# Two attention loops of a two-block network on one core: how operands of 64 and 15 rows are laid out for TensorE

## The reference

```python
def stick_breaking_attention(q, k, v):                 # q, k, v: 8 heads of 64
    for i in range(s_len // Q_BLOCK):                  # two blocks of 128 queries
        z = jnp.einsum('bhqd,bhkd->bhqk', qb, kb).astype(jnp.float32) * scale
        log_1m = jnp.where(mask, jax.nn.log_sigmoid(-z), 0.0)
        suffix = lax.cumsum(log_1m, axis=3, reverse=True) - log_1m
        a = jnp.where(mask, jnp.exp(jax.nn.log_sigmoid(z) + suffix), 0.0)
        outs.append(jnp.einsum('bhqk,bhkd->bhqd', a.astype(vb.dtype), vb))
```

```python
        logit_c = jnp.einsum('bqghd,bngd->bqghn', qt, k_cmp).astype(jnp.float32) + bias_c[None]
        p_c = jax.nn.softmax(logit_c, axis=-1) * has_any[None, :, None, None, None]
        o_c = jnp.einsum('bqghn,bngd->bqghd', p_c.astype(v_cmp.dtype), v_cmp)   # n = 15
        ...
        o = gt[..., 0:1] * o_c + gt[..., 1:2] * o_s + gt[..., 2:3] * o_w
```

## Time and profile before

| | |
|---|---|
| median of 3 runs | 1212.1 us (1211.89 to 1212.76) |
| the profiled execution | 1208.83 us, its trace spans 1207.0 us |
| PE busy with matmuls | 1192.6 us, 99% of the span |
| DVE, ACT, POOL busy | 861.1, 646.8, 216.9 us |
| the chain that ended last | 93% PE, 3% DVE, 2% DMA, 1% ACT |
| granted TensorE clock, mean | 0.998 of full speed |
| DMA | 182 GB/s over the span, queue 1 takes 49.6% of the 16 engines |
| a turn of the first head loop | 7.84 to 8.20 us |
| a turn of the NSA loop | 5.14 us |

### The profile page before, as it was taken

How to read it: one execution, slowest core, us unless ns; L and a number is a source line. 1 busy time by engine, 2 the same in 40 slices (tenths; PEclk the granted TensorE clock), 3 DMA queues, 4 the chain that set the end, 5 groups by cost and what they waited for, 6 DMA issues and landing times.

```text
span 1207.0 us, 19811 instructions
## 1 busy us (share of the span) xinstructions
PE 1192.6 (99%) x7931; PEld 1066.7 (88%) x7931; DVE 861.1 (71%) x1188; ACT 646.8 (54%) x868; POOL 216.9 (18%) x106
## 2 busy tenths in 40 slices
PE   8999999999999999999999999999999999999997
PEld 6888889988899888888999988888899879888886
DVE  6887666788767787766778777665688776766553
ACT  6655545465655665544643555544446774655441
POOL 0444300000000244310000025510000330454000
PEclk9999999999999999999999999999999999999999
DMA  8555545953335455555545555555567205555540
GB/s 301 189 210 179 205 175 179 277 208 106 105 139 185 159 210 190 185 199 181 179 163 179 194 189 208 182 202 181 201 246 268 82 1 175 210 179 203 180 170 36
DMA packets 31570, 217.55 MB, mean 180 GB/s; under 512 B 3584, under 2 KB 3856, under 8 KB 6272
## 3 DMA queue, kind: packets, MB, share of 16 engines
q1 hardware_dynamic: 30144, 210.85, 49.6%
q0 software_dynamic: 1344, 5.53, 1.6%
HBM read 215.30 MB, written 4.22 MB: 182 GB/s over the span
## 4 chain that ended last, share of the span: by engine, by line
PE 93%; DVE 3%; DMA 2%; ACT 1%; issue 0%; SPq 0%; DVEq 0%; ACTq 0%
PE bank L1514 38%; PE bank L1515 19%; PE bank L1507 9%; PE bank L1508 9%; PE bank L1509 9%; DMA raw<-weights 1%; DVE w_hl L792 1%; PE bank L1891 1%; PE bank L1603 1%; DMA h<-x_t 1%; PE bank L1605 1%; PE bank L1604 1%; ACT w_hl L405 1%; PE bank L1789 1%; PE bank L1777 0%
## 5 line engine op out<-in xcount | busy, mean ns | idle before, releaser
L792 DVE TENSOR_TENSOR w_hl<-raw,w_hl 128x2048 fp32r<-128x2048 f32 x194 | 444.0, 2289 | 117.5 <-ACT w_hl L405 116.5
L405 ACT ACTIVATE w_hl<-raw 128x2048 fp32r<-128x2048 f32 x195 | 370.4, 1902 | 116.7 <-PE bank L1515 50.8
L1514 PE MATMUL bank<-x_hl,w_hl 128*128 128x512 f32 x864 | 301.2, 394 | 1.8 <-DVE w_hl L1010 0.9
L1514 PE MATMUL bank<-hidden,w_hl 128*128 128x512 f32 x832 | 288.6, 393 | 0.0
L361 POOL TENSOR_TENSOR hidden<-hid_f,hidden 128x256 fp32r<-128x256 f32 (+1 forms) x76 | 188.1, 2474 | 525.3 <-ACT hidden L488 309.7
L1515 PE MATMUL bank<-x_hl,w_hl 128*128 128x256 f32 x864 | 240.5, 278 | 0.0
L1515 PE MATMUL bank<-hidden,w_hl 128*128 128x256 f32 x832 | 231.0, 278 | 0.0
L1514 PEld LDWEIGHTS bank<-x_hl,w_hl 128*128 128x128 f32 x864 | 161.9, 187 | 39.7 <-DVE w_hl L792 1.2
L1514 PEld LDWEIGHTS bank<-hidden,w_hl 128*128 128x128 f32 x832 | 155.9, 187 | 35.8
L1507 PE MATMUL bank<-x_hl,w_hl 128*128 128x256 f32 x576 | 164.6, 286 | 0.1
L1508 PE MATMUL bank<-x_hl,w_hl 128*128 128x256 f32 x576 | 162.9, 283 | 0.0
(11 more groups left out here) (360 smaller groups left out, 1598.6 us busy)
## 6 DMA issues: line engine op xcount, KB each, us to landing
raw<-weights SPq DMA_DIRECT2D x197, 1024.0 KB, 4.9
bias_skew<-bias_rows POOLq DMA_DIRECT2D x1, 3072.0 KB, 27.7
gate_or_bias<-bias_skew POOLq DMA_DIRECT2D x1, 2048.0 KB, 10.7
h<-x_t SPq DMA_DIRECT2D x2, 512.0 KB, 6.4
raw<-weights SPq DMA_DIRECT2D x2, 512.0 KB, 8.3
out_t<-out_g SPq DMA_DIRECT2D x4, 256.0 KB, 2.5
con<-consts SPq DMA_DIRECT2D x1, 769.5 KB, 13.5
heads<-p_t POOLq DMA_DIRECT2D x1, 256.0 KB, 2.7
```

What stands on the lines that cost most here:

```text
L405: nc.scalar.activation(dst, src, ACT.Copy).then_inc(hi_split, 1)
L792: V.tensor_tensor(w_lo[:, s, :], raw[:, s, :], w_hi[:, s, :].bitcast(F32), ALU.subtract).then_inc(lo_split, 1)
L1514: mm(out_, w_hi[:, s, c:c + m], x, start=start, stop=False, **kw)
```

## The change

Stick-breaking queries now lie in tiles of 128 partitions with zeros in the rows of the other head: even heads in `sb_q` (in `y_f`), with partitions 64 to 127 zero, odd heads in two new tiles `sb_odd`, with partitions 0 to 63 zero. The tiles `sb_odd` use memory of `y_hl` that is free at that time. The keys stay two heads to a tile. `z` of a head is then a product over all 128 partitions. POOL writes the zeros once, after the last chunk of the first feed-forward layer. DVE writes the queries with two instructions of 64 partitions in place of one of 128; the keys take a plain product with the scale. In the head loop, `z` now stands ahead of the MLA scores.

In the NSA layer `v_cmp` grows from 64 to 256 columns, filled with zeros by POOL, and group `g` writes its 15 rows in columns 64 `g` to 64 `g` + 63. Part 2 of `n_out` then uses all 128 partitions of `v_cmp` and `c_t`.

```diff
@@ -165,6 +165,8 @@
         f_at = nc.sbuf_base
         x_f, y_f = sb("x_f", [P, KT, S]), sb("y_f", [P, KT, S])
         blk_k = nc.alloc_sbuf_tensor_at("blk_k", [P, 16, 2, 64], F32R, offset=f_at)
+        sb_odd = [nc.alloc_sbuf_tensor_at(f"sb_odd{i}", [P, 2, S], F32, offset=nc.sbuf_base + (5 + 2 * i) * 2 * S * 4)
+                  for i in range(2)]
         y_hl = sb("y_hl", [P, KT, 2, S], F32R)
 
         hidden = nc.alloc_sbuf_tensor_at("hidden", [P, 2 * MF, 2, S], F32R, offset=over)
@@ -218,6 +220,7 @@
             sem("s_z"), sem("s_abs"), sem("s_min"), sem("s_ln"), sem("s_l"), sem("s_e"), sem("s_x"), sem("s_a"),
             sem("s_pv"))
         merged_done = sem("merged_done")
+        masks = sem("masks")
         ple_sig = sem("ple_sig")
         bias_ready, bias_out, bias_in = sem("bias_ready"), sem("bias_out"), sem("bias_in")
         bias_mm = sem("bias_mm")
@@ -262,7 +265,7 @@
         s_t2, s_m, s_lm = (sq_flat[:, 384 * i:384 * i + 384] for i in range(3))
         s_p = [sq_flat[:, 1152 + 384 * i:1536 + 384 * i] for i in range(2)]
 
-        v_cmp = mv[:, 0, 0:64]
+        v_cmp = mv[:, 0, 0:256]
         c_stat = mv[:, 1, 160:288].rearrange("p (a q h) -> p a q h", a=4, q=2)
 
         k_cmp = mv[:, 1, 0:64].rearrange("p (j e n) -> p j e n", j=2, e=2)
@@ -362,6 +365,10 @@
                                             ALU.subtract).then_inc(hid_lo, 1)
 
             low("ffn1")
+            pool.wait_ge(chunk_used, C["latent"])
+            nc.gpsimd.memset(sb_q[64:128, :, :], 0.0).then_inc(masks, 1)
+            for t in sb_odd:
+                nc.gpsimd.memset(t[0:64, :, :], 0.0).then_inc(masks, 1)
             pool.wait_ge(bias_ready, 1)
             pool.dma_start(bias_rows.ap(), bias_1d[:, :]).then_inc(bias_out, 16)
             pool.wait_ge(bias_out, 16)
@@ -384,6 +391,7 @@
             nc.gpsimd.memset(blk_k[:, :, :, 60:64].bitcast(F32), 0.0).then_inc(setup, 1)
             nc.gpsimd.memset(blk_v[:, :, :, 60:64].bitcast(F32), 0.0).then_inc(setup, 1)
             pool.wait_ge(op_lo, PC["blk_v"] + 1)
+            nc.gpsimd.memset(v_cmp, 0.0).then_inc(setup, 1)
             nc.gpsimd.memset(y_flat[:, 0:1024], 0.0).then_inc(setup, 1)
             for t in range(PAIRS - 1):
                 pool.wait_ge(n_fac, t + 1)
@@ -1054,8 +1062,14 @@
                 c = C["sb_q"] + j
                 dve.wait_ge(chunk_used, c + 1)
                 b = two(bank[:, TURN + (DRAIN["sb"] + j) % 3, :])
-                V.scalar_tensor_tensor(out=y_f[:, 2 * j:2 * j + 2, :], in0=b, scalar=0.125 if j < 2 else 1.0,
-                                       in1=r_two, op0=ALU.mult, op1=ALU.mult).then_inc(drained, 1)
+                if j < 2:
+                    dve.wait_ge(masks, 3)
+                    for rows, q in ((slice(0, 64), sb_q[0:64, 2 * j:2 * j + 2, :]), (slice(64, 128), sb_odd[j][64:128, :, :])):
+                        ins = V.scalar_tensor_tensor(out=q, in0=b[rows], scalar=0.125, in1=r_two[rows], op0=ALU.mult,
+                                                     op1=ALU.mult)
+                else:
+                    ins = V.tensor_tensor(y_f[:, 2 * j:2 * j + 2, :], b, r_two, ALU.mult)
+                ins.then_inc(drained, 1)
                 nxt(c)
             rsqrt("c_q", bank[:, SUMS, 0:S], width=384, r_out=r_lat[:, 0, :])
             rsqrt("c_kv", bank[:, 3, 0:S], width=256, r_out=r_lat[:, 1, :], last=r_ready)
@@ -1427,9 +1441,10 @@
                 src = bank[rows, 0, 256:288].rearrange("p (a b) -> p a b", a=2)
                 ins = V.tensor_copy(k_cmp[rows, :, e, 0:NCMP], src[:, :, 0:NCMP])
             ins.then_inc(cmp_done, 1)
+            dve.wait_ge(setup, 8)
             for g in range(4):
                 rows = slice(32 * g, 32 * g + NCMP)
-                ins = V.tensor_copy(v_cmp[rows, :], bank[rows, 0, 320:384])
+                ins = V.tensor_copy(v_cmp[rows, 64 * g:64 * g + 64], bank[rows, 0, 320:384])
             ins.then_inc(cmp_done, 1)
             nxt(PHI[3])
             n_factors(0)
@@ -1437,7 +1452,7 @@
             c_max, c_sum, c_rec, c_fac = (c_stat[:, m, :, :] for m in range(4))
             by_head = lambda ap: ap.rearrange("p (t g) -> p t g", t=4)
             dve.wait_ge(c_scores, 1)
-            dve.wait_ge(setup, 8)
+            dve.wait_ge(setup, 9)
             for q in range(2):
                 c = c_p[:, q, :, :, 0:c_n[q]]
                 first = (159, 31)[q]
@@ -1761,21 +1776,21 @@
             pe.wait_ge(normed, 1)
             for hd in range(HEADS + 1):
                 if hd < HEADS:
+                    if hd == 1:
+                        pe.wait_ge(normed, 4)
+                    if hd >= 2:
+                        pe.wait_ge(s_x, hd - 1)
+                    z = bank[:, z_bank[hd % 2], :]
+                    k = sb_k[:, hd // 2, :]
+                    q = sb_q[:, hd // 2, :] if hd % 2 == 0 else sb_odd[hd // 4][:, hd // 2 % 2, :]
+
+                    mm(z[:, 0:256], k[:, 0:128], q, start=True, stop=False, **kw)
+                    mm(z[:, 256:384], k[:, 128:256], q[:, 128:256], start=False, stop=False, **kw).then_inc(s_z, 1)
                     if hd >= 1:
                         pe.wait_ge(m_max, hd)
-                    if hd == 1:
-                        pe.wait_ge(normed, 4)
                     q, k = heads[:, hd, :], heads[:, 8 + hd, :]
                     mm(bank[:, 0, 0:128], q[:, 0:128], k[:, 0:128], start=True, stop=True)
                     mm(bank[:, 0, 128:384], q[:, 128:256], k, start=True, stop=True).then_inc(m_scores, 1)
-                    if hd >= 2:
-                        pe.wait_ge(s_x, hd - 1)
-                    z = bank[:, z_bank[hd % 2], :]
-                    r = slice(64 * (hd % 2), 64 * (hd % 2) + 64)
-                    q, k = sb_q[r, hd // 2, :], sb_k[r, hd // 2, :]
-
-                    mm(z[:, 0:256], k[:, 0:128], q, start=True, stop=False, **kw)
-                    mm(z[:, 256:384], k[:, 128:256], q[:, 128:256], start=False, stop=False, **kw).then_inc(s_z, 1)
                 if hd == 0:
                     pe.wait_ge(qk_raw, 10)
                     key_factors(2)
@@ -1931,7 +1946,7 @@
                 for part in range(5):
                     for e in range(2):
                         grp = 2 * (t // 4) + e
-                        cols, own = slice(64 * grp, 64 * grp + 64), slice(32 * grp, 32 * grp + NCMP)
+                        cols = slice(64 * grp, 64 * grp + 64)
                         nt = nsa_t[:, t % 2, e, :]
                         o = bank[64 * e:64 * e + 64, t // 2 % 2, (t % 2) * S:(t % 2) * S + S]
                         if part == 0:
@@ -1939,7 +1954,7 @@
                         elif part == 1:
                             mm(o, n_vw[:, 0, cols], nt[:, 256:512], start=False, stop=False, **kw)
                         elif part == 2:
-                            mm(o, v_cmp[own, :], c_t[own, (t % 4) * S:(t % 4) * S + S], start=False, stop=False, **kw)
+                            mm(o, v_cmp[:, cols], c_t[:, (t % 4) * S:(t % 4) * S + S], start=False, stop=False, **kw)
                         elif part == 3:
                             mm(o[:, 128:256], n_vs[:, 1, cols], nt[:, 512:640], start=False, stop=False, **kw)
                         else:
```

## The result

The changed kernel took 1205.84 us, the median of 4 runs (1203.34 to 1207.38). The kernel before, on the same chip, took 1211.99 (4 runs, 1211.48 to 1212.76). The ratio is 0.9946, with a 95% interval of 0.9926 to 0.9966. The forecast was 1206.9. The profiled execution took 1207.38 us, its trace spans 1205.6, the mean granted clock was 0.998.

The account below looks back on a forecast made before the run. PE, busy 1192.6 of 1207.0 us, was taken to set the pace. Savings of 3.0 (`z`) and 2.2 us (compressed values) gave 5.2, hence 1206.9 us from 1212.1; range 1205.5 to 1208.5, widened to 1204.5 to 1210.0 for 8 in 10.

Parts of the forecast that it names:

- What bounds: Whole kernel: PE, busy 1192.6 of 1207.0 us, waits for nobody in the two loops and sets the pace.
- the 1.4 of the forecast: Queries on DVE: two 64-partition instructions replace one, twice; 1.4 us more DVE time, cost to the kernel 0.
- 0.10 us on the last step and 0.10 on the first: PE in the head loop: each change of array form adds 0.10 us on either side, 0.20 together.
- `z`: 3.0 forecast: First head loop, stick-breaking scores over 128 rows: 0.40 us less in heads 1 to 7, 0.20 in head 0.
- Compressed values: NSA outputs, 128 rows: 0.29 us less per turn, 2.3 us over eight turns, 2.2 after allowed waiting.
- The 0.1 allowed for waiting in the last turns: NSA loop, last two turns: 0.1 us of PE waiting because they draw on DVE, taking 2.3 to 2.2.
- the 0.1 us that the prediction set as its limit: Both loops, trace after: PE should show no wait of more than 0.1 us.
- Order: First head loop, `z` ahead of the MLA scores: costs nothing, `z` ends some 0.85 us earlier in a turn.
- the cover in turn 4: First head loop, ACT's end to PE's outputs: 1.34 us would shrink to 0.42, still positive, costed at nothing.
- NSA covers 0.27: NSA loop: POOL's cover and ACT's idle time, 0.56 us each, would each shrink to 0.27 per turn.
- Third rival: Full-row loads exposed before `z`: 6.1 us, plus up to 1 in NSA outputs; time 1214.0; chance 0.05.
- The sum: Both loops on PE: 3.0 + 2.2 = 5.2 us saved, profiled execution 1203.6, median 1206.9 us.

Follow-up runs that it names:

- e7: The kernel before with MLA and `z` score products mixed (MLA, `z`, MLA, `z`), `z` over 64 rows; median 1214.91 us, ratio 1.0036 to the kernel before.
- e8: The changed kernel with MLA and `z` score products mixed, `z` over 128 rows; median 1206.9 us, ratio 0.9963 to the kernel before.
- e1: The changed kernel measured again with no edit; median 1206.11 us, ratio 0.9947 to the kernel before.
- e2: The changed kernel with compressed values back in their own 15 rows, only the scores part kept; median 1208.14 us, ratio 0.9973 to the kernel before.
- e4: The changed kernel with NSA keys, hence NSA scores, also over 128 zero-filled rows; median 1216.22 us, ratio 1.0038 to the kernel before.
- e5: The changed kernel in the old order, MLA scores ahead of `z`, still 128 rows; median 1205.84 us, ratio 0.995 to the kernel before.
- e3: The changed kernel with first-loop queries and order as before, only the compressed values part kept; median 1209.77 us, ratio 0.9985 to the kernel before.
- e6: The kernel before with only the order changed, `z` (64 rows) ahead of the MLA scores; median 1210.84 us, ratio 0.9985 to the kernel before.

## Why the prediction was right

- **What bounds: right.** PE has the only path. In the first loop what it lost in steps it lost in time one to one; in the second the steps gave 2.38 us, and waits took 0.23 back. The scalings of queries and keys take DVE 4.1 us where they took 2.7, the 1.4 of the forecast (the page has 2.0 in all), and POOL has 2.1 more (forecast about 2.3); neither costs PE anything: from the relative bias to the key factors ahead of the first head loop, the stretch in which DVE scales the queries, it is 68.1 or 68.2 us in all ten profiles, with the split instructions and without.
- **0.10 us on the last step and 0.10 on the first: right.** After, the steps have their widths alone; e7 shows both extras added on one step, e8 that the operands have no part.
- **`z`: 3.0 forecast, 2.9 measured** in the trace after, in e1, e2, e4, e5 and e8 (loop 74.7 to 71.8). Heads 1 to 7 give 0.39 each and head 0 0.19. In e7 two more changes a head cost 0.39, the price of the 0.40 that went.
- **Compressed values: 2.2 forecast, 2.15 measured** (34.7 to 32.6, in e1, e3, e5 and e8 too). A turn is 0.30 shorter, eight of them 2.38, where the forecast had 2.3. The 0.1 allowed for waiting in the last turns was mis-sized: it was 0.23, most of it the wait for DVE's copy L1429. So the part comes out close because two small errors cancel. This is also the one place where PE shows a new wait of more than the 0.1 us that the prediction set as its limit.
- **Order: no cost, right; the cover in turn 4 was mis-sized.** The place that the prediction calls the outputs of head 4 is turn 4, which computes the outputs of head 3. Forecast 0.42 us, measured 0.78. Counted from the matmuls of the relative bias (202.59 before, 206.14 after), PE reaches them 1.75 us sooner (forecast 1.8), DVE starts its work at head 1 0.95 sooner (0.88), and ACT ends 1.19 sooner, not 0.88. The term that was mis-sized is the last: I took DVE's chain from head 1 on as rigid, and it gave another 0.24 us; why isn't shown. In e5 (201.96) the same three are 1.73, 0.37 and 0.61, again 0.24 between the last two. Without the new order I would have put the cover at 0.26 below nothing (1.34 - 1.8 + 0.20), and it was 0.22 above. It was also not the place with the least cover: turn 3 has 0.68 after and 0.10 in e5, so the margin of the old order was thinner than this reading shows.
- **NSA covers 0.27: right** for POOL and ACT, 0.25 and 0.26. DVE's copy L1429 in the last turn was not looked at: it had 0.53 us of cover before and has none after.
- **Third rival, exposed loads: false here.** L1788 starts 0.53 behind L1787 and L1792 0.23 behind that, with no gap for a load of 0.19 us. The products in full rows cost what their widths ask.
- **The sum: 5.2 forecast, 5.05 by the places.** The runs give 6.2 for this pair, 6.4 in e1, 6.1 in e5 and 4.5 in e8, whose intervals all hold 5.05. That three of them say more I do not count as the change's. The profiled time was forecast as 1203.6 and came out at 1207.38: the 3.8 us are nearly all the 3.5 of the first stage.
- **The range was too narrow, and that the median fell into it owes something to luck.** The 0.4 us for the scatter between runs came from three runs within 0.9 us. The four runs after spread over 4.0 us, the 29 before on e1's chip over 7.2, and a stage that the change doesn't touch moved by 3.5. Single runs of kernels with both parts lie between 1203.06 and 1209.74 us, outside the range of 1205.5 to 1208.5 on either side; the medians 1205.84, 1206.11, 1205.84 (e5) and 1206.9 (e8) all lie in it.

## What to carry to other kernels

Where PE sets the end, read the starts of its matmuls and not its busy share, and compare each step with what its width asks: the excess at each change of array form is a price per change. Filling rows with zeros to avoid a change paid here where no second product ran beside the small one in other rows: `z` stands alone, and the two heads of the compressed values lie side by side in columns, which full rows leave as it is. Where two products shared the array in disjoint rows, full rows took their concurrency away and cost more than the changes (2.69 us for 1.50). A cover is to be read in every turn and for every engine that PE waits for, and a short wait shows only in the steps from start to start: idle time misses it where the last matmul is still on its way. A gain smaller than the scatter of the runs is read from the stages of two traces, and the stages that the change does not touch are read as well.

## What the hardware showed that I had not expected

**Two paces of the first feed-forward layer.** Groups of PE's matmuls between 80 and 140 us of the span (busy us, mean ns, idle), before and then after:

```profile
L1514 PE MATMUL bank<-x_hl,w_hl 128*128 128x512 f32 x160 | 55.5, 391 | 0.0
```

```profile
L1529 PE MATMUL bank<-x_hl,w_hl 128*128 128x512 f32 x164 | 58.0, 399 | 0.0
```

The same groups, 710 to 780 us, before and then after:

```profile
L1514 PE MATMUL bank<-x_hl,w_hl 128*128 128x512 f32 x203 | 70.4, 394 | 0.0
```

```profile
L1529 PE MATMUL bank<-x_hl,w_hl 128*128 128x512 f32 x203 | 70.4, 394 | 0.0
```

In the first layer a pair of matmuls (512 and 256 columns) takes 0.3467 us from start to start in one pace and 0.3533 in the other, through the whole layer; 528 pairs by 0.0066 make 3.5 us. The second layer has 0.3466 to 0.3468 in every profile. The granted clock is at its upper level (1.00, 2.4 GHz) in both. The slow pace stood in the profiles of after, e1, e4, e6, e7 and e8, the fast one in before, e2, e3 and e5. e6 and e7 are the kernel before but for a few lines behind this stage, and e5 is the changed kernel but for order, so it does not go with the change. What chooses the pace stays open. Its 3.5 us are near the size of the scatter between runs, 4 to 7 us; single runs without a profile don't tell which pace they had.

**A clock that fell behind very narrow matmuls.** Timeline of PE in e1, the second of the NSA scores (turn 1, ahead of the loop), and then windows of the same trace (us; busy and count of PE, PEld, DVE, ACT, POOL; granted clock; DMA share; GB/s):

```profile
947.31 2.61 PE L1906 MATMUL bank<-heads 64*128 64x256 f32 x12
949.85 0.58 PE L1618 MATMUL bank<-w_hl,x_hl 128*128 128x256 f32 x1
```

```profile
944.00:948.00 4.00, 4.00 (x36) 3.86 (x37) 1.97 (x3) 2.56 (x3) 4.00 (x2) 0.96 0.93 338
948.00:950.00 2.00, 2.00 (x11) 1.19 (x7) 1.67 (x6) 0.55 (x2) 0.17 (x1) 0.50 0.88 373
```

PE is busy throughout. The 3.6 us ahead of L1906 hold 32 matmuls of 14 and 30 columns (L2038). Then the granted clock is 0.50, the level of 1.2 GHz, and the 12 matmuls of L1906 take 2.54 us, start to start, for 1.50. The stage that holds it took 29.0 to 29.1 us in e1, e3, e5 and e6, and 27.5 or 27.6 in before, after, e2, e7 and e8: 1.6 us, whatever the kernel. So an engine that is busy by the page, with matmuls this narrow, can still stand ahead of a fall of its clock. That they bring the fall about isn't shown: the same 32 matmuls stand there in the other six profiles, where the clock stays at 1.00.
